# Delta rule scan: 32x32 inverses built from 16x16 ones in fixed steps; row scalings and diagonal blocks written by ScalarE

## The reference

```python
diff = G[..., :, None] - G[..., None, :]
decay = jnp.where(incl, jnp.exp(jnp.where(incl, diff, 0.0)), 0.0)
A = jnp.where(strict, jnp.einsum('nbhid,nbhjd->nbhij', kb, kc) * decay, 0.0)
sol = lax.linalg.triangular_solve(A + I, rhs, left_side=True, lower=True, unit_diagonal=True)
u, w = sol[..., :dv], sol[..., dv:]
def step(S, xs):                      # over the chunks, forward and backward
    v_new = u_c - w_c @ S
    o = q_c @ S + qk_c @ v_new
    S = gl * S + k_c^T @ v_new
```

## Time and profile before

| what | us |
|---|---|
| three timed runs, median (lowest, highest) | 4786.62 (4784.84, 4792.46) |
| the profiled execution: device time | 4793.38 |
| the profiled execution: span | 4791.5 |
| of it: scan, from the first `vn(0)` copy to the first `vn(9)` copy | 235.46 |

### The profile page before, as it was taken

The page is one execution under the profiler, slowest core; times in us unless marked ns, Lnnn a source line. Parts: engine busy times, 40 slices in busy tenths (PEclk is TensorE's granted clock), DMA queues, the critical chain, the costliest instruction groups (busy, mean ns, idle before and its releaser), DMA issues.

```text
span 4791.5 us, 45095 instructions
## 1 busy us (share of the span) xinstructions
PE 4363.4 (91%) x18086; PEld 3027.9 (63%) x18086; DVE 2344.3 (49%) x3763; ACT 1394.4 (29%) x2615; POOL 992.4 (21%) x767
## 2 busy tenths in 40 slices
PE   7895789988999999988899998989888888999998
PEld 3455754757888888655454455555565657888886
DVE  2778974254555653344432027564667644333334
ACT  3462221132111111332311015351554533222222
POOL 2114635111433441034331000001000011000001
PEclk9997899999999999988889999999999999999999
DMA  5112243011433431220201110011000031111111
GB/s 189 49 53 82 71 142 104 27 70 53 117 104 106 114 110 42 69 72 27 79 27 32 39 37 29 26 60 50 20 20 16 29 106 44 44 53 44 44 44 62
DMA packets 255712, 300.41 MB, mean 63 GB/s; under 512 B 19040, under 2 KB 209904, under 8 KB 254224
## 3 DMA queue, kind: packets, MB, share of 16 engines
q1 hardware_dynamic: 236016, 218.76, 14.9%
q0 software_dynamic: 17408, 75.64, 5.1%
q10 hardware_dynamic: 2080, 3.15, 0.2%
HBM read 267.42 MB, written 30.09 MB: 62 GB/s over the span
## 4 chain that ended last, share of the span: by engine, by line
PE 62%; DVE 9%; ACT 5%; issue 1%; POOL 1%; DMA 1%; POOLq 0%; DVEq 0%; ACTq 0%
PE bank L193 60%; PE bank L196 2%; DVE Mx L205 1%; ACT Mx L202 1%; ACT at21P L202 1%; ACT at20P L202 1%; POOL sq L205 1%; DVE at21sm L223 1%; DVE at20sm L223 1%; DVE x L211 0%; DMA wslot<-in_w_in 0%; DVE wfl L205 0%; DVE at11sm L223 0%; DVE at10sm L223 0%; DVE at21Pl L205 0%
## 5 line engine op out<-in xcount | busy, mean ns | idle before, releaser
L193 PE MATMUL bank<-h,wslot 128*128 128x512 f32 (+3 forms) x2096 | 899.3, 573 | 33.1 <-DMA wslot<-in_w_in 19.3
L193 PEld LDWEIGHTS bank<-h,wslot 128*128 128x128 f32 (+1 forms) x2096 | 383.7, 191 | 378.8 <-issue 361.3
L193 PE MATMUL bank<-hT,wslot 128*128 128x512 f32 (+3 forms) x1136 | 464.2, 566 | 15.5 <-DVE hT L211 7.3
L193 PEld LDWEIGHTS bank<-hT,wslot 128*128 128x128 f32 (+1 forms) x1136 | 213.0, 190 | 242.5 <-issue 237.4
L193 PE MATMUL bank<-ffn1h,wfh 128*128 128x512 f32 x704 | 280.5, 398 | 10.2 <-DVE ffn1l L211 9.2
L193 PE MATMUL bank<-ffn2h,wgh 128*128 128x512 f32 x704 | 276.2, 392 | 10.0 <-DVE ffn2l L211 9.5
L211 DVE SCALAR_TENSOR_TENSOR x<-bank,mod,x 128x512 f32<-128x512 f32 x224 | 164.4, 746 | 244.6 <-PE bank L193 244.2
L193 PE MATMUL bank<-ffn1l,wfh 128*128 128x512 f32 x704 | 276.0, 392 | 0.0
L193 PE MATMUL bank<-ffn1h,wfl 128*128 128x512 f32 x704 | 275.6, 391 | 0.0
L193 PE MATMUL bank<-ffn2l,wgh 128*128 128x512 f32 x704 | 274.7, 390 | 0.0
L193 PE MATMUL bank<-ffn2h,wgl 128*128 128x512 f32 x704 | 274.6, 390 | 0.0
(11 more groups left out here) (533 smaller groups left out, 8863.4 us busy)
## 6 DMA issues: line engine op xcount, KB each, us to landing
wslot<-in_w_in SPq DMA_DIRECT2D x40, 1024.0 KB, 5.5
ffn1t<-in_w_mod POOLq DMA_DIRECT2D x64, 512.0 KB, 4.7
wslot<-in_w_ffn_in SPq DMA_DIRECT2D x44, 512.0 KB, 5.4
Mx<-acsT SPq DMA_DIRECT2D x32, 512.0 KB, 4.8
at1w<-in_ada_w POOLq DMA_DIRECT2D x24, 512.0 KB, 4.7
wslot<-in_ffn_w_gate SPq DMA_DIRECT2D x22, 512.0 KB, 4.0
wslot<-in_ffn_w_up SPq DMA_DIRECT2D x22, 512.0 KB, 5.3
wslot<-in_w_ffn_out SPq DMA_DIRECT2D x20, 512.0 KB, 5.2
```

The source lines that it names most:

```text
L193: return Counted() if counting[0] else self.q.matmul(o, l, r, start=start, stop=stop)
```

## The change

- **Inverses.** `sub` inverts the two 16x16 diagonal blocks of a 32x32 block at once in 15 pieces (a fourth dimension of 2, made by the distance of 528 elements; `ktok` grows by 96 elements for it). The lower left 16x16 block then comes as -X2 A21 X1: four pieces of a product and a `reduce_sum` for T = A21 X1 and four for X2 T, in a scratch `big` of 1024 elements (`Ah[1]` for batch 0, a new tile for the others). A batch now has 31 pieces.
- **Pace.** In the scan a step takes a fixed number of pieces: 12, 8, 41 (all that is left), 4, 8, 8, 41, then none; two at a time while more than 20 are allowed. Batch 1 begins at s = 0 and ends in s = 2; batch 2 begins at s = 3 and ends in s = 6.
- **ACT in place of POOL.** `chunk(s+1)` for all steps, and `diagonal(s+2)` for steps from 2 on, leave POOL. ACT does `kd` and `vb` as four 128x128 copies with a per-partition scale each, and `Dm` and `DT` as four 32-partition copies each, for each d. The order in ACT's list of a step: `vn(s)`, `decay` (s = 0, 3), `begin(s+2)`, `chunk(s+1)`, `diagonal(s+2)`. POOL keeps the first two diagonals (which write the zeros too), `one` and the queries. The waits of PE, DVE and SP follow.

The whole of `sub`'s new part and of ACT's and DVE's new lists:

```diff
-        for j in range(31):
-            m, w = 31 - j, j + 1
+        A2, R2 = diag16(Ah[B % 2]), diag16(Rh)
+        for j in range(15):
+            m, w = 15 - j, j + 1
+            t = rt_[:, 0:2 * m * w].rearrange("p (h i c) -> p h i c", h=2, c=w)
...
+        big = big0 if B == 0 else big1
+        T = rt_[:, 256:512].rearrange("p (i c) -> p i c", c=16)
+        for q in range(0, 16, 4):
+            n = 16 - q
+            t = big[:, 0:64 * n].rearrange("p (i c k) -> p i c k", c=4, k=n)
+            e.wait_ge(*d.now())
+            e.tensor_tensor(t, grid(A)[:, 16:32, q:16].unsqueeze(2).to_broadcast([128, 16, 4, n]),
+                            grid(Rb)[:, q:16, q:q + 4].rearrange("p k c -> p c k").unsqueeze(1).to_broadcast([128, 16, 4, n]),
+                            OP.mult).then_inc(d("tm", B, q), 1)
+            e.wait_ge(*d.now())
+            e.reduce_sum(T[:, :, q:q + 4], t).then_inc(d("t", B, q), 1)
+            yield
+        for q in range(0, 16, 4):
+            n = q + 4
...
+            e.reduce_sum(grid(Rb)[:, 16 + q:20 + q, 0:16], t).then_inc(d("x", B, q), 1)
             yield
...
+        def diagonal(s, d):
...
+            e.wait_ge(*gs.dve.after("Z", B))
+            e.wait_ge(*gs.pool.after("DT", 1, d))
+            e.wait_ge(*gs.pe.after("pt", s - 2, d))
+            for name, o, t in (("Dm", Dm, rows), ("DT", DT, cols)):
+                if name == "DT":
+                    e.wait_ge(*gs.dve.after("u", s - 2, d))
+                for q in range(4):
+                    e.activation(blocks(o[s % 2][d][:, :])[quarter(q), :, q, :], in_place(t, u, q),
+                                 AF.Copy).then_inc(gs.act(*((name, s, d, q) if q < 3 else (name, s, d))), 1)
+
+        def chunk(s):
+            for d in range(2):
+                col = gcol(s, d)
+                e.wait_ge(*kb_in[d].after(s))
+                if s:
+                    e.wait_ge(*gs.pe.after("st", s - 1, d))
+                for x in range(4):
+                    e.activation(kd[d][:, hs[x]], kb[d][:, hs[x]], AF.Copy, scale=kdf[:, col + x:col + x + 1]).then_inc(gs.act(*(("kd", s, d, x) if x < 3 else ("kd", s, d))), 1)
+                e.wait_ge(*vb_in[d].after(s))
+                for x in range(4):
+                    e.activation(vb[d][:, hs[x]], vb[d][:, hs[x]], AF.Copy, scale=bet[:, col + x:col + x + 1]).then_inc(gs.act(*(("vb", s, d, x) if x < 3 else ("vb", s, d))), 1)
...
-            if s in (0, 2):
+            if s in (0, 3):
                 decay(e, 1 if s == 0 else 2)
             if s < 8:
                 begin(s + 2)
+            if s < 9:
+                chunk(s + 1)
+            if s < 8:
+                for d in range(2):
+                    diagonal(s + 2, d)
...
         for s in range(10):
-            k = 2 if s < 2 else 1
-            if s in (0, 2):
-                more(41)
+            left = [(12, 8, 41, 4, 8, 8, 41, 0, 0, 0)[s]]
+            if s in (0, 3):
                 pieces = sub(e, 1 if s == 0 else 2)
                 more(4)
```

More of the change, by code:

```diff
@@ L665, in build @@
     gc_out, gr_in = Sem("gcT", 16), [Sem(f"gr{i}", 16) for i in range(2)]
-    pre = [ktok[:, i * 1024:(i + 1) * 1024] for i in range(5)]
-    Wd, Ab, Rb = [W0[:, :]] + pre[0:2], pre[2:4], pre[4]
+    pre = [ktok[:, i * 1024:(i + 1) * 1024] for i in range(2)] + [ktok[:, 2048 + i * 1056:2048 + (i + 1) * 1056] for i in range(3)]
+    Wd, Ah, Rh = [W0[:, :]] + pre[0:2], pre[2:4], pre[4]
+    Ab, Rb = [a[:, 0:1024] for a in Ah], Rh[:, 0:1024]
     E, rt_ = sqr.bufs[0:2], sqr.bufs[2]
@@ L696, in unit, with made @@
         return d * 16 + batch_chunks(s // 4, d).index(order[d][s]) * 4
+    def made(s):
+        return gs.act if s >= 2 else gs.pool
     def quarter(b):
@@ L773, in sub @@
         if B == 2:
-            e.wait_ge(*gs.pool.after("DT", 3, 1))
+            e.wait_ge(*gs.act.after("DT", 3, 1))
         e.wait_ge(*ks_out.after("out"))
@@ L834, in gp_sp @@
         e.wait_ge(*gp.dve.after("kt", 8))
-        e.dma_start(io["kspill"].rearrange("(c p) x -> p c x", p=128), ktok[:, :].rearrange("p (c x) -> p c x", x=512)).then_inc(ks_out("out"), 16)
+        e.dma_start(io["kspill"].rearrange("(c p) x -> p c x", p=128), ktok[:, 0:NC * 512].rearrange("p (c x) -> p c x", x=512)).then_inc(ks_out("out"), 16)
         load(e, ("qkv", 4), [(w1, 0, 8, 4 * 256, 256, 0)])
@@ L1191, in chunk @@
                 if s:
-                    e.wait_ge(*gs.pool.after("kd", s - 1, d))
+                    e.wait_ge(*gs.act.after("kd", s - 1, d))
                     e.dma_start(kb[d][:, :], io["kspill"][c * 128:(c + 1) * 128, :]).then_inc(kb_in[d](s), 16)
@@ L1233, in pt @@
                 e.wait_ge(*gs.dve.after("kkE", s, d))
-                e.wait_ge(*gs.pool.after("Dm", s, d))
+                e.wait_ge(*made(s).after("Dm", s, d))
                 four("pt", s, d, kkE[s % 2][d], Dm[s % 2][d])
@@ L1239, in v1 @@
                 e.wait_ge(*gs.dve.after("pt", s, d))
-                e.wait_ge(*gs.pool.after("DT", s, d))
+                e.wait_ge(*made(s).after("DT", s, d))
                 four("v1", s, d, PT[d], DT[s % 2][d])
@@ L1275, in gs_pe @@
                 e.wait_ge(*gs.dve.after("u", s, d))
-                e.wait_ge(*(gs.dve.after("r", s, d) if s else gs.pool.after("vb", s, d)))
+                e.wait_ge(*(gs.dve.after("r", s, d) if s else gs.act.after("vb", s, d)))
                 four("vn", s, d, Va[d], vb[d])
@@ L1280, in gs_pe @@
                 for d in range(2):
-                    e.wait_ge(*gs.pool.after("kd", s, d))
+                    e.wait_ge(*gs.act.after("kd", s, d))
                     e.wait_ge(*gs.act.after("vn", s, d))
@@ L1320, in begin @@
                     e.activation(qds[s % 2][d][:, :], b[:, :], AF.Exp).then_inc(gs.act("qd", s, d), 1)
+        def diagonal(s, d):
+            B, u = s // 4, unit(s, d)
+            rows, cols = (Ab[B % 2], Wd[B]) if d == 0 else (Wd[B], Ab[B % 2])
+            e.wait_ge(*gs.dve.after("Z", B))
[18 more added lines that the diff above has]
+                    e.activation(vb[d][:, hs[x]], vb[d][:, hs[x]], AF.Copy, scale=bet[:, col + x:col + x + 1]).then_inc(gs.act(*(("vb", s, d, x) if x < 3 else ("vb", s, d))), 1)
         for i in range(2):
@@ L1371, in rest @@
             e.wait_ge(*gs.pe.after("ks", s, d))
-            e.wait_ge(*gs.pool.after("vb", s, d))
+            e.wait_ge(*gs.act.after("vb", s, d))
             for x in range(4):
@@ L1415, in more, with some @@
                 next(pieces, None)
+        def some():
+            n = min(left[0], 2 if left[0] > 20 else 1)
+            left[0] -= n
+            more(n)
         for s in range(10):
-            k = 2 if s < 2 else 1
-            if s in (0, 2):
-                more(41)
+            left = [(12, 8, 41, 4, 8, 8, 41, 0, 0, 0)[s]]
+            if s in (0, 3):
                 pieces = sub(e, 1 if s == 0 else 2)
@@ L1427, in gs_dve @@
                     pt(s + 1, d)
-                more(k)
+                some()
             for d in range(2):
@@ L1442, in gs_dve @@
                     plus("v2", s + 1, d, Vb)
-                more(k)
+                some()
+            if s in (2, 6):
+                more(41)
             if s < 8:
@@ L1448, in gs_dve @@
                     plus("u", s + 1, d, Va)
-                    more(1)
+                    some()
     def gs_pool(e):
@@ L1469, in diagonal @@
             e.tensor_tensor(blocks(DT[s % 2][d][:, :]), spread(cols, u), msk, OP.mult).then_inc(gs.pool("DT", s, d), 1)
[L1471 to L1479, removed]
         def queries(s):
@@ L1499, in gs_pool @@
                 one(e, 1)
-            if s == 2:
+            if s == 3:
                 one(e, 2)
-            if s < 9:
-                chunk(s + 1)
             if s < 8:
-                for d in range(2):
-                    diagonal(s + 2, d)
                 queries(s + 2)
```

19 lines of the change are left out of this document (14 added, 5 removed).

## The result

| | before | after |
|---|---|---|
| median of 20 timed runs (lowest, highest), us | 4787.03 (4784.84, 4792.46) | 4779.55 (4775.27, 4786.79) |
| profiled execution, device time | 4793.38 | 4782.53 |
| its span | 4791.5 | 4780.7 |
| first `vn(0)` copy | 396.84 | 399.35 |
| first `vn(9)` copy | 632.30 | 623.92 |

The ratio is 0.9984, 95% interval 0.9977 to 0.9991: faster, by 7.5 us on the medians, or 0.16%. That is inside the stated range, 4.6 us above the 4775 that was forecast. By the prediction's bound of 0.2% it counts as no change, the case that had a chance of 0.35.

What follows compares the result with a forecast made beforehand. DVE was taken to bound scan cycles 0 to 4 and PE 5 to 7; -13.1 us in cycles 0 to 7 and +1.4 at the ends make -11.7, from 4786.6 to 4775 us, range 4757 to 4795.

Steps and rivals of the forecast that it cites:

- What bounded the kernel before: Scan cycles 0 to 4 bound by DVE, 5 to 7 by PE; POOL's work leaving frees some 26 us of DVE.
- The loop on ACT: From one `vn` copy through gate rows, `begin`, scalings and diagonal copies to the next: no cycle with a diagonal under about 24 us.
- plain cycles: Scan cycles 3, 4 and 7: 24.3 us each forecast, 23 to 26 us as the sign of being right.
- The cycles with pieces: Scan cycles 1, 2, 5 and 6, carrying inverse pieces on DVE: 25.5, 30.5, 26.3 and 27.8 us.
- The new inverse: DVE time of one batch alone: 24 us taken, of 22.1 to 28.9, against 23.0 before; no gain by itself.
- Rival 2: Products and sums on DVE slow, 1.70 ns per element, 29 us a batch: 4786 us, no change; chance 0.20.
- The start: Ahead of the scan: batch 0's pieces delay its start by 1.1 to 4 us, +2 taken, less 1.1 for `kkE(1)`.
- The ninth cycle: Last scan cycle, with a scaling but no diagonal, hidden behind the load of `vb`: +0.5 us for PE's clock.
- At the end of the scan: Total gain: cycles 0 to 7 -13.1 us, start and ninth cycle together +1.4, so -11.7 us.
- The signs: Plain cycles 23 to 26 us, ACT busy near 16, `pt` waiting for `Dm`, substitution instructions 0.2 to 0.3 us, POOL's share a third.
- 1 (a shorter chain): ACT's chain shorter, DVE alone decides: cycles 0 to 7 take 195 us, with the ends 4761; chance 0.22.
- 3 (the clock falls in every cycle): PE idles for `Dm`, falls to 1.2 GHz each time and becomes the bound: cycles 229 us, 4797 in all; chance 0.08.

Runs made afterwards that it cites:

- e3: The changed kernel with the 31 row steps of the old 32x32 substitution put back (39 pieces, own pace): 4778.8 us, ratio 0.9976 to the kernel before.
- e7: The changed kernel with the products' second operand read from neighbouring elements, not 64 or 128 bytes apart (results no longer the reference's): 4775.2 us, one run.
- e8: The changed kernel with gate rows issued first and ACT's list reordered to vn, E, kd, qd, vb, Dm, DT: 4757.9 us, ratio 0.9935 to the kernel before.

## Why the prediction was right, point by point

- **What bounded the kernel before**: this held. e3 against before shows 28.7 us of DVE's time given back by the work that left POOL, where 26 were worked out. Cycles 0 to 4 fell by 32.5 us together (36.2 forecast), and cycles 5 to 7 rose by 21.6 (23.1 forecast).
- **The loop on ACT**: the mechanism held, with its place, in cycles 0, 3, 4 and 7. The terms, worked out and measured in cycle 4, are: gate rows 7.6 and 7.55; `begin` 4.8 and 4.72; scalings 4.7 and 4.68; twelve copies 4.7 (3.5 to 4.9) and 5.24; half of `pt` and of `vn` 2.2 and 3.93. The sums are 24.0 and 26.1. The mis-sized step is the choice of clock: the text named 1.9 us more if the clock falls, and 26 for the cycle, and then took 24.3. It fell each time. The plain cycles 3, 4 and 7, forecast at 24.3, came at 27.6, 26.1 and 25.6. These 6.4 us are three times the miss of the whole sum, 2.2. Cycle 0 took 26.0 where 24.3 was forecast. In cycle 3 the gate rows came 1.5 us later than in cycle 4; the wait for them ended with the load there too, and why the load was later stays open.
- **The cycles with pieces**: forecast 25.5, 30.5, 26.3 and 27.8 for cycles 1, 2, 5 and 6, measured 24.3, 28.5, 25.8 and 25.5, so the forecast was 5.9 too long together. DVE was busy 22.2, 28.1, 21.7 and 25.2 in them, and not 25, 30.5, 26.5 and 28. How much of that is POOL's remaining stretch, counted at 1 to 2 us per cycle, and how much is work that falls across the edge of a cycle, I did not separate. The two misses nearly cancel: 207.3 forecast, 209.5 measured. That is luck: the sum was better than its terms.
- **The new inverse**: 24 us a batch was taken, of 22.1 to 28.9. Measured in the scan, substitution 9.2, products 10.3 and sums 6.6 are 26.1, and 46 gaps of 0.03 make 27.5. The surcharge belonged to the products and not to the sums. The nearest row for a sum, 1.905 us, reads at a distance, and the text took its price for that of short groups; the sums here read neighbours and cost 1.22 us for 1024 elements. The products read at a distance and cost 1.9 us. The Trainium skill's page "SBUF — State Buffer", section "Door 1: The DMA port swizzle", says that accesses that cross to a new 16-byte line each time pay a penalty, without a size for it. e7 agrees, with 1.96 us at a distance and 1.226 together. Rival 2 was half right in its mechanism: products slow, sums not. It did not decide: its 2 us more in each of the cycles 1, 2, 5 and 6 did not come, and taking the distance away shortens the sum by 3.5 us (e7).
- **The start**: the taps began at 367.02 (364.5 to 367.5 forecast), the last `vtok` copy ended at 377.84 (375.3 to 378.3), +3.7 where +2 was taken. `kkE(1)` took 1.28 us and not 2.43, as forecast. `kkE(0)` took 2.68 in place of 1.58, which was not foreseen, but DVE's wait for PE behind it shrank from 1.74 to 0.41 us. The first `vn` copy came 2.5 later, forecast +0.9.
- **The ninth cycle**: 15.10 both times, forecast +0.5.
- **At the end of the scan** the change had gained 8.4 us (632.30 to 623.92), forecast 11.7. The rest of the span is 4159.2 us before and 4156.8 after, and between 4150.5 and 4161.7 in the ten experiments, none of which touches it. This scatter is as large as the effect; the median of 7.5 agrees with the 8.4 of the scan. The profiled execution, 4782.5, came within 0.8 us of its 4781.7, while the median came 4.6 above its 4775: the first is luck, since scan and rest miss in opposite directions. The range of 38 us was wide against a change of 7.5, so that the time fell inside it says less than the terms do.
- **The signs**: POOL's work in the nine cycles fell to a third (133.6 to 45.5 us), `pt` waited for ACT's `Dm`, and the substitution's instructions took 0.29 and 0.32 us on the mean. The plain cycles were to be 23 to 26 us and two of the three were longer, and ACT was busy 17 to 18 us and not 16.
- **Rivals.** 1 (a shorter chain) fell: cycle 4 took 26 us and not 22.8. Its cycles of 195 with the ends make 4763 and not 4761. 3 (the clock falls in every cycle) was right that it falls, and wrong on how far it reaches: the mean granted clock stayed at 0.82 to 0.94, and PE did not become the bound. Its own terms give 230 us or more, not 229.

## What to carry to other kernels

Work moved to an idle engine joins that engine's list: write down the list for one step with the wait that stands in it, and ask whether its last item releases its first. Here ACT was 78% idle in the cycles before the change and still became the loop. Moving the issue of the gate rows and reordering ACT's list (e8) was worth another 0.49%, three times the change itself. When a term is taken from a loop, look at which buffer's release stands behind it before you count the gain.

## What the runs showed of the hardware that I had not expected

- A two-input instruction on DVE that reads one operand 64 to 128 bytes apart takes 1.91 to 2.02 us for 1024 elements here, 1.226 when the operand lies together. A sum over 1024 neighbouring elements in groups of 16 takes 1.22; a sum of 1024 elements read at a distance takes 1.905.
- A 32-partition copy on ACT between strided SBUF and a plain row takes 0.44 us when four follow each other, no less than the 0.40 of the same size out of PSUM. Copies of 128x128 with a scale follow each other at 0.29.
- Two waits of PE of 3.47 and 2.40 us with 1.1 us of work between them left the granted clock at 0.50 for the matmuls behind them.
